# q, k and v projected from resident high and low halves, 256 columns at a time, with two tiles of the threshold search on ScalarE

## What is computed

```
h = rmsnorm(x); proj = h @ w_in          # q, k, v (512 each), iq, ik, iw, glu, gates
q = rmsnorm(q per head) * q_norm_g; k = rmsnorm(k per head) * k_norm_g
score = sum_h relu(iq_h . ik) * iw_h     # -inf where not admissible
sel = top_k(score, 256)                  # attention is over these keys only
A = softmax(q k^T / 8 + bias) v  @ w_attn_out
u = ga_in * sigmoid(gb_in); c = depthwise_conv31(u) + b
B = silu(layernorm(c)) @ w_conv_out
x += (sigmoid(ga) * A + sigmoid(gc) * B) @ w_out
x += (silu(h2 @ w_gate) * (h2 @ w_up)) @ w_down,  h2 = rmsnorm(x)
```

## Time and profile before

| | |
|---|---|
| median of 3 runs | 2078.76 us (2072.36, 2078.76, 2079.02) |
| the profiled execution | 2071.23 us, span 2069.3 us |
| granted TensorE clock, mean | 0.975 |
| busy over the span: PE, DVE, ACT, POOL | 94%, 55%, 31%, 18% |
| chain that ended last | PE 83%, POOL 5%, DVE 4%, issue 4%, ACT 3% |

### The profile page before, as it was taken

One profiled execution on the slowest core, in us unless ns is written; L12 is line 12 of the kernel. 1 busy time (PEld: TensorE's weight loads), 2 busy tenths in 40 slices (PEclk: granted clock), 3 DMA queues, 4 the chain that ended last, 5 costly groups with the idle time before them and its releaser, 6 DMA issues.

```text
span 2069.3 us, 26437 instructions
## 1 busy us (share of the span) xinstructions
PE 1935.9 (94%) x10080; PEld 1549.9 (75%) x10080; DVE 1138.4 (55%) x1700; ACT 637.5 (31%) x1161; POOL 377.6 (18%) x331
## 2 busy tenths in 40 slices
PE   6968999999888986898999989999999999999998
PEld 3533899999433433566994459999999999999997
DVE  1054899999999946776442233333343333433333
ACT  2244322221233126676101122322233222322232
POOL 1101122664477802341000000000000000000000
PEclk9998999999999997999999999999999999999999
DMA  6340112321331253673522223333343333433332
GB/s 204 89 75 20 62 42 76 95 97 57 138 132 61 82 173 96 217 258 149 190 99 92 81 81 111 130 124 122 122 153 122 122 125 131 163 129 122 122 122 101
DMA packets 86606, 242.37 MB, mean 117 GB/s; under 512 B 14549, under 2 KB 32373, under 8 KB 77315
## 3 DMA queue, kind: packets, MB, share of 16 engines
q1 hardware_dynamic: 81643, 227.34, 32.4%
q10 hardware_dynamic: 4896, 14.16, 1.7%
HBM read 211.68 MB, written 26.61 MB: 115 GB/s over the span
## 4 chain that ended last, share of the span: by engine, by line
PE 83%; POOL 5%; DVE 4%; issue 4%; ACT 3%; SPq 1%; DMA 1%; POOLq 0%; DVEq 0%; ACTq 0%
PE ps L642 20%; PE ps L640 20%; PE ps L641 20%; PE ps L966 6%; PE ps L670 4%; PE ps L788 4%; DVE buf L1390 2%; POOL buf L1774 2%; PE ps L863 1%; PE ps L840 1%; POOL buf L1782 1%; PE ps L882 1%; PE ps L823 1%; PE ps L722 1%; PE ps L853 1%
## 5 line engine op out<-in xcount | busy, mean ns | idle before, releaser
L640 PE MATMUL ps<-buf,buf 128*128 128x384 f32 (+2 forms) x2220 | 771.6, 348 | 8.8 <-DVE buf L1339 7.5
L642 PE MATMUL ps<-buf,buf 128*128 128x384 f32 (+2 forms) x2220 | 773.9, 349 | 0.0
L641 PE MATMUL ps<-buf,buf 128*128 128x384 f32 (+2 forms) x2220 | 772.5, 348 | 0.0
L640 PEld LDWEIGHTS ps<-buf,buf 128*128 128x128 f32 x2220 | 418.2, 188 | 28.3 <-DVE buf L1339 5.7
L641 PEld LDWEIGHTS ps<-buf,buf 128*128 128x128 f32 x2220 | 418.5, 188 | 17.9
L642 PEld LDWEIGHTS ps<-buf,buf 128*128 128x128 f32 x2220 | 418.0, 188 | 18.0
L1339 DVE TENSOR_TENSOR buf<-buf,buf 128x1024 fp32r<-128x1024 f32 (+4 forms) x216 | 301.3, 1397 | 176.4 <-ACT buf L1317 39.0
L1641 DVE TENSOR_TENSOR buf<-buf,ps 128x384 f32<-128x384 f32 x66 | 36.6, 555 | 401.6 <-PE ps L642 401.6
L1403 DVE TENSOR_SCALAR_CACHE_REDUCE buf<-buf,buf 128x384 uint8<-128x384 f32 (+6 forms) x231 | 218.3, 1009 | 1.2
L1446 DVE SCALAR_TENSOR_TENSOR buf<-buf,buf,buf 128x1024 f32<-128x1024 f32 x210 | 200.6, 996 | 3.7
L788 PE MATMUL ps<-buf,buf 128*128 128x512 f32 x432 | 193.5, 605 | 4.2 <-DMA buf<-hT_scr 4.2
(11 more groups left out here) (169 smaller groups left out, 1659.3 us busy)
## 6 DMA issues: line engine op xcount, KB each, us to landing
buf<-in_w_ffn SPq DMA_DIRECT2D x67, 1024.0 KB, 5.7
buf<-in_w_ffn SPq DMA_DIRECT2D x66, 512.0 KB, 3.6
buf<-in_cache_k SPq DMA_DIRECT2D x16, 1024.0 KB, 7.5
buf<-in_cache_v SPq DMA_DIRECT2D x16, 1024.0 KB, 10.2
buf<-hT_scr SPq DMA_DIRECT2D x27, 512.0 KB, 3.4
buf<-in_w_cols SPq DMA_DIRECT2D x24, 512.0 KB, 4.4
buf<-in_x SPq DMA_DIRECT2D x18, 512.0 KB, 5.0
gate_scr<-buf ACTq DMA_DIRECT2D x16, 576.0 KB, 5.4
```

What stands on the lines that cost most here:

```text
L640: mm(dst, whi, xhi, start=start, stop=False)
L641: mm(dst, whi, xlo, start=False, stop=False)
L642: return mm(dst, wlo, xhi, start=False, stop=stop)
```

## The change

Stage 4 uses `hhi` and `hlo`, which stay in SBUF: the copies to and from `hT_scr` go. q, k and v are projected by halves of 256 columns (`HW`), as three products: 54 units q (36 for k and q, `NQK`, 18 for v) of 24 matmuls. The weights of each half are split by ACT (`qkv_high`) and POOL (`qkv_low`, 128x2048). The head norm is spread: ACT squares a unit in one operation (`squares`), DVE sums it per head (`head_sums`), POOL scales, adds and takes the power (`inverse_norm`), DVE multiplies from PSUM (`scale_heads`), POOL multiplies by the gain (`gain`). DVE's 109 taps are divided: 58 ahead of these units, 24 between them (in two units of three), 27 behind.

Stage 3 gives the two largest tiles (1024 and 1152 keys) to ACT, which takes the sum of the sign of (threshold - score) with one activation each (`sign_step`), ahead of an evacuation, in 8 groups of 9. Behind the 32 steps DVE raises these two thresholds where needed to the least score above them, and counts again. The convolution's accumulator moves to the place of `scoreS`, so the taps now wait until the mask is in `mask_scr`. POOL takes two taps instead of one in three of the column tiles. Buffers move accordingly; `hT` and `vN` get another layout.

```diff
+HW = AW // 2
+NQK, NQ = 4 * NT, 6 * NT
...
+        acc = scoreS
...
+            def qkv_in(f):
+                sp.dma_start(wraw_[f], A["w_qkv"][f // 2][:, :, HW * (f % 2):HW * (f % 2) + HW]).then_inc(S(f"wqkv_in{f % 2}"), 16)
+
+            qkv_in(0)
...
+            for t in range(12, NCOL):
+                sp.wait_ge(S("col_done"), NG * (t - 3))
+                col_in(t // 4, t % 4)
+                if t == 17:
+                    sp.wait_ge(S("mask_made"), NSEL)
+                    sp.dma_start(A["mask_scr"], scoreS).then_inc(S("mask_out"), 16)
+
             sp.wait_ge(S("col_done"), NG * NCOL)
-            for c in range(3):
-                copy_h(c, 0, c == 0)
-                if c == 0:
-                    sp.dma_start(wqkv[1], A["w_qkv"][1]).then_inc(S("wqkv_in1"), 16)
-                if c == 1:
-                    sp.dma_start(wqkv[0], A["w_qkv"][2]).then_inc(S("wqkv_in0"), 16)
-                with sp.Fori(1, NG) as i:
-                    copy_h(c, i, False)
+            qkv_in(1)
+            sp.wait_ge(S("qkv_done"), NT)
+            qkv_in(2)
+            sp.wait_ge(S("conv_made"), 2)
+            sp.wait_ge(S("out_state"), 48)
+            sp.wait_ge(S("qkv_done"), NT + 1)
+            qkv_in(3)
+            sp.wait_ge(S("qkv_done"), 3 * NT)
+            qkv_in(4)
+            sp.wait_ge(S("qkv_done"), 4 * NT)
+            qkv_in(5)
...
+            def turn(q):
+                pe.wait_ge(S("qn_made"), q + 1)
+                if q >= 3:
+                    pe.wait_ge(S("turn_made"), q - 2)
+                for p in range(2):
+                    l = nc.tensor.transpose(bank(4 + q % 3)[:, p * P:(p + 1) * P], qn[:, q % 3, p * P:(p + 1) * P], ident)
                 l.then_inc(S("qk_turned"), 1)
 
-            def project(c, i, before):
-                for j in range(3):
-                    n = c * NT + i * 3 + j
-                    pe.wait_ge(S(f"hs_in{j}"), (c * NG + i + 1) * 16)
-                    if not (c == 0 and before is None):
-                        pe.wait_ge(S("qkv_evac"), n - 2)
-                    for k in range(KD):
-                        l = mm(bank(j), hs[:, j, k], wqkv[c % 2][:, k], start=k == 0, stop=k == KD - 1)
-                    l.then_inc(S("qkv_done"), 1)
-                    if j == 0 and before is not None:
-                        bc, bt = before
-                        if bc < 2:
-                            turn(bc, bt, 2, bc == 0 and isinstance(bt, int) and bt < 3)
-                    if j > 0 and c < 2:
-                        turn(c, i * 3 + j - 1, j - 1, c == 0 and before is None)
-
-            for c in range(3):
-                pe.wait_ge(S(f"wqkv_in{c % 2}"), 16 * (c // 2 + 1))
-                project(c, 0, None if c == 0 else (c - 1, NT - 1))
-
-                if c == 0:
-                    project(c, 1, (c, 2))
-                    project(c, 2, (c, 5))
+            def project(q):
+                f, t = divmod(q, NT)
+                if t == 0:
+                    pe.wait_ge(S("qkv_split"), f + 1)
+                if q < NQK:
+                    if q >= 4:
+                        pe.wait_ge(S("scaled"), q - 3)
+                elif f == 4:
+                    if t < 8:
+                        pe.wait_ge(S("scaled"), NQK - 3 + t // 2)
+                    else:
+                        pe.wait_ge(S("turn_made"), NQK - 2)
+                elif t < 3:
+                    pe.wait_ge(S("turn_made"), NQK)
                 else:
-                    with pe.Fori(1, NG) as i:
-                        project(c, i, (c, i * 3 - 1))
-
-            pe.wait_ge(S("qkv_evac"), 3 * NT)
-            pe.wait_ge(S("turn_made"), 2 * NT)
+                    pe.wait_ge(S("vN_made"), t - 2)
+                for k in range(KD):
+                    mm(qkv_bank(q), hhi[:, t, k], wqhi[f][:, k], start=k == 0, stop=False)
+                    mm(qkv_bank(q), hhi[:, t, k], wqlo[f][:, k], start=False, stop=False)
+                    l = mm(qkv_bank(q), hlo[:, t, k], wqhi[f][:, k], start=False, stop=k == KD - 1)
+                l.then_inc(S("qkv_done"), 1)
+
+            for q in range(NQ):
+                project(q)
+                if 3 <= q < NQK + 3:
+                    turn(q - 3)
...
+            def sign_step(g):
+
+                step = g - g // 9
+                if g % 9 == 8 or step >= 32:
+                    return
+                act.wait_ge(S("thr_made"), step + 1)
+                for j, (n, (sc, L)) in enumerate(signed):
+                    if step or j:
+                        act.wait_ge(S("signs_made"), NSIGN * step + j)
+                    ac(signs[:, 0:L], sc, ACT.Sign, scale=-1.0, bias=thrf[:, n:n + 1], accum_out=cnt[:, n:n + 1])\
+                        .then_inc(S("signs_made"), 1)
...
+                        sign_step(t * NG + c)
...
+            def squares(q):
+                act.wait_ge(S("qkv_done"), q + 1)
+                if q >= 3:
+                    act.wait_ge(S("ssq_made"), q - 2)
+                ac(sqn[:, q % 3], qkv_bank(q), ACT.Square).then_inc(S("squared"), 1)
...
+            def count(op, tiles):
+
+                for j, (n, (sc, L)) in enumerate(tiles):
+                    if j >= 2:
                         ch.wait(1)
-                    ch.add(ve.tensor_scalar(hits[n % 2][:, 0:L], sc, thrf[:, n:n + 1], None, op, ALU.add,
+                    ch.add(ve.tensor_scalar(hits[j % 2][:, 0:L], sc, thrf[:, n:n + 1], None, op, ALU.add,
                                             accum_out=cnt[:, n:n + 1]))
                 ch.wait()
 
+            tiles = list(enumerate(select))
+            own, other = slice(0, NSEL - NSIGN), slice(NSEL - NSIGN, NSEL)
+            for j, (n, (sc, L)) in enumerate(signed):
+                ch.add(ve.memset(kvec[:, j:j + 1], float(L - 2 * TOPK)))
             dve.wait_ge(S("score_done"), NSEL)
-            ch.link(ve.memset(thr, 0))
+            ve.memset(thr, 0).then_inc(S("thr_made"), 1)
+            dve.wait_ge(S("thr_made"), 1)
             for bit in range(31, -1, -1):
-                count(ALU.is_ge)
-                ch.link(ve.tensor_scalar(flip, cnt, float(TOPK), -1.0 if bit == 31 else float(1 << bit),
-                                         ALU.is_lt, ALU.mult))
+                count(ALU.is_ge, tiles[own])
+                value = -1.0 if bit == 31 else float(1 << bit)
+                ch.add(ve.tensor_scalar(flip[:, own], cnt[:, own], float(TOPK), value, ALU.is_lt, ALU.mult))
+                dve.wait_ge(S("signs_made"), NSIGN * (32 - bit))
+                ch.link(ve.tensor_tensor(diff, cnt[:, other], kvec, ALU.subtract))
+                ch.link(ve.tensor_scalar(flip[:, other], diff, 0.0, value, ALU.is_gt, ALU.mult))
                 if bit:
-                    ch.link(ve.scalar_tensor_tensor(thr, thr, 1 << (bit - 1), flip, ALU.bitwise_xor, ALU.bitwise_xor))
+                    ve.scalar_tensor_tensor(thr, thr, 1 << (bit - 1), flip, ALU.bitwise_xor, ALU.bitwise_xor)\
+                        .then_inc(S("thr_made"), 1)
+                    dve.wait_ge(S("thr_made"), 33 - bit)
                 else:
                     ch.link(ve.tensor_tensor(thr, thr, flip, ALU.bitwise_xor))
 
-            count(ALU.is_gt)
+            count(ALU.is_gt, tiles)
+            dve.wait_ge(S("u_made"), 2 * CT)
+            for j, (n, (sc, L)) in enumerate(signed):
+                ch.link(ve.tensor_scalar(raised[:, 0:L], sc, thrf[:, n:n + 1], 3e38, ALU.is_le, ALU.mult))
+                ch.link(ve.tensor_tensor_reduce(raised[:, 0:L], raised[:, 0:L], sc, 1.0, 3e38, ALU.add, ALU.min,
+                                                least[:, j:j + 1]))
+            ch.link(ve.tensor_scalar(diff, cnt[:, other], float(TOPK), None, ALU.is_ge))
+            ch.link(ve.tensor_tensor(least, least, diff, ALU.mult))
+            ch.link(ve.tensor_scalar(diff, diff, 1.0, 3e38, ALU.subtract, ALU.mult))
+            ch.link(ve.tensor_tensor(least, least, diff, ALU.add))
+            ch.link(ve.tensor_tensor(thrf[:, other], thrf[:, other], least, ALU.max))
+            count(ALU.is_gt, tiles[other])
...
+            dve.wait_ge(S("mask_out"), 16)
+            conv_order = [0, CT - 1, *range(1, CT - 1)]
...
+            def head_sums(q):
+                r = slice(4 * (q % 3), 4 * (q % 3) + 4)
+                dve.wait_ge(S("squared"), q + 1)
+                if q >= 3:
+                    dve.wait_ge(S("rsq_made"), q - 2)
+                ve.tensor_reduce(ssq[:, r], sqn[:, q % 3].rearrange("p (h d) -> p h d", h=4), AX.X, ALU.add)\
+                    .then_inc(S("ssq_made"), 1)
+
+            def scale_heads(q):
+                r = slice(4 * (q % 3), 4 * (q % 3) + 4)
+                dve.wait_ge(S("rsq_made"), q + 1)
+                if q >= 3:
+                    dve.wait_ge(S("qn_made"), q - 2)
+                ve.tensor_tensor(raw[:, q % 3].rearrange("p (h d) -> p h d", h=4),
+                                 qkv_bank(q).rearrange("p (h d) -> p h d", h=4),
```

(53 more changed lines are left out.)

270 lines of the change are left out of this document (112 added, 158 removed).

## The result

The changed kernel takes **2111.2 us** (median of 4 runs, 2108.0 to 2112.7) where before took 2078.4 beside it: a ratio of 1.0167, 95% interval 1.0146 to 1.0187, so **slower by 1.7%, some 33 us**. I had forecast slower by 11 us (2090), with a range of 2046 to 2122. The direction came out, to which I had given 0.50, and so did the mechanism: DVE's string of operations ends last, and POOL's operations hold it up. The size did not.

What follows compares the result with a forecast made beforehand. PE was taken to bound the stretch before attention, with DVE under 15 us behind. DVE's new queue would end at 765 us, starting attention 11 us later: 2078.8 + 11 = 2090 us, range 2046 to 2122 (8 in 10).

Steps and rivals of the forecast that it cites:

- PE gains: Projections of q, k and v: a product of 256 columns takes 0.117 us, 64 us less on PE alone.
- Columns: Column projections on PE end at 555 us instead of 522, a 33 us loss hidden by DVE's 58 taps.
- 10 us beyond the mask: PE's gap before column tile 18 lasts until 10 us behind the mask.
- The string sets the end: DVE's queue from search to last taps ends last, at 765 us, so attention starts 11 us later.
- 58 taps: DVE's convolution taps ahead of the head norm: 1.94 us each, 113 us, and 3 us of copies and the sum.
- The counts and the raising: Behind the search: a count of seven, raising two thresholds, a count of two; 15 us, 17 with collisions.
- The mask: Making the mask on DVE takes 44 us as before; it is ready at 470 us instead of 523.
- The search: 32 threshold steps, 4.9 us each when clean; 186 us in all (172 to 200), against 256 with the last count.
- (a): In the search, ACT's signs wait for POOL's `u_made` in GLU tiles 2, 4 and 6: 8 us.
- (b): In the search, small DVE operations are held while POOL runs a two-input operation: 20 us (bounds 6 and 34).
- Units: 36 units of k and q at 2.9 us each, plus 20 us for four `qkv_low`: 124 us (bounds 104 and 145).
- Rival 1: DVE and POOL hardly collide along DVE's queue: attention starts 33 us early, 2046 us; chance 0.33.

Runs made afterwards that it cites:

- e1_mask_late: Changed kernel with the mask's DMA moved from between the weights of column tiles 17 and 18 to between 19 and 20: 2108.7 us.
- e2: Changed kernel with 13 of POOL's 15 convolution taps left out: 2067.4 us.
- e3: Changed kernel with 46 taps ahead of the 36 units and one in each unit, instead of 58 ahead and one in two of three: 2095.1 us.
- e6: Changed kernel with POOL's 15 convolution taps moved to DVE: 2090.9 us.
- e8: Changed kernel with the memset of `biasS` and its two waits moved from ahead of DVE's last 27 taps to behind five of them: 2104.8 us.
- e10: Changed kernel with POOL's 24 `col_low` cut from 1024 to 128 columns, PE multiplying the high part twice: 2069.8 us.
- e11: Changed kernel with POOL's first 11 `col_low` in the columns waiting for DVE's next threshold, to lie beside counts: 2090.8 us.
- e4: Changed kernel without ACT's signs: all seven tiles counted on DVE, nothing raised, mask's DMA ahead of tile 22's weights: 2116.5 us.
- e12: Changed kernel with all taps on DVE (48 ahead of units, 44 in them, 32 behind), memset behind five taps, `col_low` beside counts: 2044.6 us.

## Why the prediction was right on the sign and wrong on the size

- *PE gains*: right. 0.12 us a product (forecast 0.117), so the weight load adds nothing at 256 columns either, which the rows of before could not tell. The gain is worth nothing, since PE stands still for 32 us in front of the units.
- *Columns*: "10 us beyond the mask" held (PE's tile 18 at 492.4, mask 482.3), and the loss was hidden, as e1_mask_late showed.
- *The string sets the end*: right. e2, e3, e6, e8, e10 and e11 shortened DVE's string and attention followed; e1 brought PE's q, k and v forward by 15 us and it did not.
- *The failed step* is the price of POOL's operations along the string, in its item "58 taps" above all: "beside `col_low` and POOL's own taps no row shows it, and I take 1.94". The rows behind 1.94 were of POOL's head norm operations beside taps. With their copies the taps took 129.3 us where I had 116. At 1.58 us a tap they would be 95, so the collisions cost 35 us where I had 21. The counts and the raising took 22.0 us against 17 (14.9 in e2, without POOL's taps: 7 us of collisions where I had 2). The mask took 46.4 against 44 (36.1 in e4, with nothing beside it: 10 us, where the row of before that I copied held 8). Together with the search these are 23 of the 29 us, after 2 us that the mask's DMA gave back.
- *The search* itself was nearly right: 189.6 us against 186. e12, with `col_low` beside counts and no POOL taps, took 159.3, and I had 158 for a clean one (32 x 4.9 is 157). So (a) and (b) are 30 us together, where I had 8 and 20. How they split wasn't measured.
- *Why it was too small*: the fact was already in the earlier trace rows, a DVE operation stopped until a two-input POOL operation ended. I priced it per search step and took a mean from elsewhere for the taps, instead of counting POOL's two-input operations along the whole string (24 `col_low`, 15 taps of POOL with 14 adds). The runs price each of these two groups at some 40 us. So the term was of the right kind: 82 us by the four pieces above (30 + 7 + 10 + 35), where the forecast held 59 (28 + 2 + 8 + 21).
- *Units*: 124 was close (129 to the last evacuation). The 7.8 us wait at the memset I had put at 5.
- *Rival 1* (hardly any collision) has its opposite shown: e12, which avoids them by place and by engine, ended at 2044.6. That this is near rival 1's 2046 is luck: e12 also has its taps divided in another way.

What stays open: no run removed both groups with nothing else changed. The two runs that removed one each add up to 79 us, and the four pieces to 82, so the groups seem to add, but each piece is compared with another run.

## What to carry to other kernels

Before you give one engine's spare time to another, list POOL's two-input operations and what DVE does beside each: in this kernel every one of them cost DVE's two-input and tiny operations its remaining length, and cost DVE's counts with an accumulator nothing. Tie such a POOL operation to an event that starts a long stretch of such counts; if there is none, and DVE ends last, doing the work on DVE may be cheaper. And a change that relieves the bounding engine by moving work onto the engine with 15 us of slack has to be judged on the second engine's queue, waits included, not on the first one's saving.
